# RWKV layer of a fused four-mixer kernel: another order for the first pairs' steps beside the projection, and for the solve's rows in the pair loop

## The reference

```python
r, k, v, g = jnp.einsum('pbsd,pdf->pbsf', xs[:4], w_in)
w_log = -jax.nn.softplus(-(w0 + jnp.tanh(xw @ w1) @ w2)) - 0.5
a = jax.nn.sigmoid(a0 + (xa @ a1) @ a2)
kk = kk / jnp.maximum(jnp.linalg.norm(kk, axis=-1, keepdims=True), 1e-12)
k = k * (1.0 + (a - 1.0) * k_a)
def step(state, inp):
    r_t, w_t, k_t, v_t, kk_t, a_t = inp
    sk = jnp.einsum('bhvk,bhk->bhv', state, kk_t)
    state = state * w_t[:, :, None, :] - sk[..., None] * (kk_t * a_t)[:, :, None, :] + v_t[..., None] * k_t[:, :, None, :]
    return state, jnp.einsum('bhvk,bhk->bhv', state, r_t)
bonus = jnp.sum(rh * kh * r_k, axis=-1, keepdims=True) * vh
```

## Time and profile before

| | |
|---|---|
| runs of the kernel before | 3641.15, 3643.06, 3659.37 us; median 3643.06 |
| the profiled execution | 3642.96 us, its span 3641.3 us |
| PE busy in the span | 3447.9 us, 95% |
| DVE, ACT, POOL busy | 1989.7, 1702.4, 252.7 us |
| granted TensorE clock, mean | 0.975 |

### The profile page before, as it was taken

One profiled execution on the slowest core, in us unless ns is written; L12 is line 12 of the kernel. 1 busy time (PEld: TensorE's weight loads), 2 busy tenths in 40 slices (PEclk: granted clock), 3 DMA queues, 4 the chain that ended last, 5 costly groups with the idle time before them and its releaser, 6 DMA issues. The chain is left out here.

```text
span 3641.3 us, 48005 instructions
## 1 busy us (share of the span) xinstructions
PE 3447.9 (95%) x18610; PEld 2851.4 (78%) x18610; DVE 1989.7 (55%) x3850; ACT 1702.4 (47%) x3234; POOL 252.7 (7%) x194
## 2 busy tenths in 40 slices
PE   7999898999998999999899899999899999999999
PEld 6888646877886777777787688888778888888887
DVE  3144343354335686775434477777864566666562
ACT  3222363265444454543324466666642765665530
POOL 0011130000001122212000000000100000000100
PEclk9999999999999999999899999999999999999899
DMA  4333403112232222222411111111222211111231
GB/s 146 121 128 128 167 1 127 41 64 81 96 107 88 73 59 62 67 56 53 148 57 42 51 36 36 36 36 36 78 86 70 93 35 41 41 36 47 70 110 47
DMA packets 219482, 263.70 MB, mean 72 GB/s; under 512 B 62716, under 2 KB 143092, under 8 KB 218232
## 3 DMA queue, kind: packets, MB, share of 16 engines
q1 hardware_dynamic: 219256, 260.63, 22.2%
HBM read 190.58 MB, written 69.99 MB: 72 GB/s over the span
## 5 line engine op out<-in xcount | busy, mean ns | idle before, releaser
L332 PE MATMUL bank<-wh,XH 128*128 128x512 f32 x1344 | 536.2, 399 | 13.2 <-DVE wl L316 9.5
L332 PE MATMUL bank<-wh,XL 128*128 128x512 f32 x1344 | 528.2, 393 | 0.0
L332 PE MATMUL bank<-wl,XH 128*128 128x512 f32 x1344 | 528.1, 393 | 0.0
L2706 PE MATMUL bank<-XH,wh 128*128 128x512 f32 x1040 | 424.5, 408 | 10.1 <-DVE wl L2695 9.6
L2706 PE MATMUL bank<-XH,wl 128*128 128x512 f32 x1040 | 408.7, 393 | 0.0
L2706 PE MATMUL bank<-XL,wh 128*128 128x512 f32 x1040 | 408.2, 392 | 0.0
L332 PEld LDWEIGHTS bank<-wh,XH 128*128 128x128 f32 x1344 | 255.7, 190 | 65.9 <-issue 10.3
L316 DVE TENSOR_TENSOR wl<-raw,wh 128x1024 fp32r<-128x1024 f32 x128 | 160.9, 1269 | 266.7 <-ACT wh L307 265.9
L332 PEld LDWEIGHTS bank<-wl,XH 128*128 128x128 f32 x1344 | 255.3, 190 | 54.3
L332 PEld LDWEIGHTS bank<-wh,XL 128*128 128x128 f32 x1344 | 255.9, 190 | 50.4
L332 PE MATMUL bank<-XH,wh 128*128 128x512 f32 x704 | 280.9, 399 | 6.8 <-DVE XL L1598 6.0
(11 more groups left out here) (441 smaller groups left out, 6902.0 us busy)
## 6 DMA issues: line engine op xcount, KB each, us to landing
sc_zt<-stage SPq DMA_DIRECT2D x88, 256.0 KB, 2.0
raw<-in_att_w_in SPq DMA_DIRECT2D x33, 512.0 KB, 4.2
raw<-in_even_w_in SPq DMA_DIRECT2D x32, 512.0 KB, 5.2
raw<-in_odd_w_in SPq DMA_DIRECT2D x32, 512.0 KB, 4.6
raw<-in_rec_w_in SPq DMA_DIRECT2D x32, 512.0 KB, 4.0
sc_h<-H SPq DMA_DIRECT2D x24, 512.0 KB, 2.6
sc_z<-stage SPq DMA_DIRECT2D x40, 256.0 KB, 2.0
z<-sc_z SPq DMA_DIRECT2D x8, 1024.0 KB, 5.6
```

Of the source, the lines that this page charges most:

```text
L332: done = e.matmul(out, lhsT, rhs, start=k == 0 and j == 0, stop=k == NK - 1 and j == 2)
L2706: done = e.matmul(bank[:, :], x[:, k, :], y[:, k, ts], start=k == 0 and j == 0, stop=k == NK - 1 and j == 2)
```

## The change

No arithmetic changes, and no DMA or instruction is added or removed. Two tables are rewritten; POOL's product inside `key` gets a step name of its own, `grow`, which stands right behind `key` wherever `key` stood, so that POOL's order stays as it was.

Beside the projection: `keys` of pair 0 goes from slot 2 to 0, its `scan` from 2 to 3 (behind `norm`), `lora` 0 of pair 1 from 8 to 5, `pack` 1 from 8 to 7, `bonus` of pair 0 from 10 to 11, `load` of pair 1 from 10 to 11, `centre` of pair 1 from 12 to 11. The solve's rows of pair 0 stood 5, 7, 7, 7, 5 in slots 9 to 13 and stand 4, 11, 1, 3, 7, 5 in slots 8 to 13.

In the pair loop: the rows stood 1, 4, 1, 3, 4, 2, 3, 6, 3, 4 at positions 5, 6, 7, 8, 9, 10, 11, 13, 14, 15 and stand 1, 4, 3, 5, 2, 3, 4, 9 at 5, 6, 8, 9, 10, 11, 13, 14. `bonus` goes behind the four rows of position 6, and `gates` from 7 to 6.

```diff
-    6: ((-1, 'tail', 1, 5), (1, 'bonus'), (1, 'solve', 4)),
-    7: ((1, 'solve', 1), (0, 'gates')),
+    6: ((-1, 'tail', 1, 5), (1, 'solve', 4), (1, 'bonus'), (0, 'gates'), ),
+    7: (),
...
-    13: ((1, 'solve', 4), (0, 'tail', 0, 1), (1, 'solve', 2)),
-    14: ((2, 'norm'), (1, 'solve', 3)),
-    15: ((0, 'tail', 0, 2), (1, 'solve', 4)),
+    13: ((1, 'solve', 4), (0, 'tail', 0, 1), ),
+    14: ((2, 'norm'), (1, 'solve', 3), (1, 'solve', 2), (1, 'solve', 4), ),
+    15: ((0, 'tail', 0, 2), ),
...
-        if what == "key":
+        if what == "grow":
             e.wait_ge(*self.scaled.at("rate", p))
             e.tensor_tensor(k, k, t, ALU.mult).then_inc(*self.key.up("k", p))
```

More of the change, by code:

```diff
@@ L1724 @@
 PLACED = {
[L1725 to L1730, removed]
-    6: ((-1, 'tail', 1, 5), (1, 'bonus'), (1, 'solve', 4)),
-    7: ((1, 'solve', 1), (0, 'gates')),
[L1733 to L1736, removed]
+    0: ((1, 'rh'), (1, 'alike', 1), (-1, 'tail', 1, 0), ),
+    1: ((-1, 'tail', 1, 1), ),
+    2: ((1, 'alike', 2), (-1, 'tail', 1, 2), (1, 'rkr'), ),
+    3: ((1, 'alike', 3), ),
+    4: ((1, 'pack', 0), (-1, 'tail', 1, 3), ),
+    5: ((-1, 'tail', 1, 4), (1, 'pack', 1), (2, 'load'), (1, 'solve', 1), ),
+    6: ((-1, 'tail', 1, 5), (1, 'solve', 4), (1, 'bonus'), (0, 'gates'), ),
+    7: (),
+    8: ((2, 'lora', 0), (1, 'solve', 3), ),
+    9: ((1, 'solve', 5), ),
+    10: ((2, 'keys'), (1, 'solve', 2), ),
+    11: ((0, 'tail', 0, 0), (2, 'lora', 1), (2, 'scan'), (1, 'solve', 3), ),
     12: (),
-    13: ((1, 'solve', 4), (0, 'tail', 0, 1), (1, 'solve', 2)),
-    14: ((2, 'norm'), (1, 'solve', 3)),
-    15: ((0, 'tail', 0, 2), (1, 'solve', 4)),
+    13: ((1, 'solve', 4), (0, 'tail', 0, 1), ),
+    14: ((2, 'norm'), (1, 'solve', 3), (1, 'solve', 2), (1, 'solve', 4), ),
+    15: ((0, 'tail', 0, 2), ),
     16: (),
[L1742 to L1748, removed]
+    17: ((1, 'unpack'), (2, 'spread'), (0, 'tail', 0, 3), (2, 'centre'), ),
+    18: ((2, 'unit'), ),
+    19: ((2, 'key'), (2, 'grow'), (2, 'exps'), ),
+    20: ((0, 'tail', 0, 4), ),
+    21: ((2, 'be'), (2, 'al'), ),
+    22: ((2, 'ka'), (0, 'tail', 0, 5), ),
+    23: ((2, 'values'), (2, 'alike', 0), ),
 }
@@ L1803 @@
 HALVES = (slice(0, 512), slice(512, 1024))
[L1807 to L1817, removed]
+BESIDE = {
+    -4: ((0, 'load'), ),
+    -1: ((0, 'begin'), (0, 'tables'), ),
+    0: ((0, 'lora', 0), (0, 'keys'), ),
+    1: ((0, 'lora', 1), ),
+    2: (),
+    3: ((0, 'norm'), (0, 'spread'), (0, 'scan'), (0, 'centre'), ),
+    4: ((0, 'unit'), (0, 'key'), (0, 'grow'), ),
+    5: ((0, 'exps'), (1, 'lora', 0), (0, 'be'), (0, 'al'), ),
+    6: ((0, 'alike', 0), (0, 'alike', 1), (0, 'alike', 2), (0, 'alike', 3), (0, 'pack', 0), ),
+    7: ((0, 'pack', 1), ),
+    8: ((0, 'rest'), (0, 'values'), (0, 'blank'), (0, 'ka'), (0, 'rh'), (0, 'rkr'), (0, 'solve', 4), ),
+    9: ((0, 'solve', 11), ),
+    10: ((0, 'solve', 1), (1, 'lora', 1), ),
+    11: ((0, 'solve', 3), (1, 'keys'), (1, 'scan'), (1, 'load'), (1, 'centre'), (0, 'bonus'), ),
+    12: ((0, 'solve', 7), (1, 'norm'), (1, 'spread'), ),
+    13: ((0, 'solve', 5), (0, 'unpack'), (1, 'unit'), ),
+    14: ((1, 'key'), (1, 'grow'), (1, 'exps'), ),
+    15: (),
+}
+PROLOGUE = ((1, 'values'), (0, 'gates'), (0, 'tokens', 0), (0, 'scores', 0), (0, 'level', 0, 'X'), (0, 'level', 0, 'G'), (0, 'level', 0, 'Y'), (0, 'level', 0, 'F'), (1, 'be'), (1, 'al'), (1, 'ka'), (1, 'alike', 0), )
 def rwkv_beside():
```

## The result

The kernel after takes 3629.26 us (median of 13 runs, 3620.31 to 3633.39), beside 3646.19 for the kernel before on the same chip. By the medians that is 16.9 us. The ratio of the means is 0.9946, 95% interval 0.9932 to 0.9959: 0.54% faster, 19.7 us of 3643. In a second comparison (`after_again`) it was 0.9956 [0.9941, 0.9971]. The profiled execution took 3621.33 us and is the second fastest of the 13.

A forecast was written before the change was run, and what follows sets the result against it. PE, busy 95% of the span, was taken to bound the kernel through its idle time beside the projection and in the pair loop. 12.1 + 1.2 + 5.8 = 19.1 us off 3642.96 gave 3624, range 3612 to 3638.

The forecast's parts named there:

- Beside the projection: Ahead of the pair loop: `unit` of pair 1 starts 12.1 us earlier, and 1.2 us of clock come back behind it.
- DVE's queue: Beside the projection: DVE needs 24.45 us from 1171.0, the end of `rkr`, to the floor of pair 1, at 1195.4.
- POOL's hold: Beside the projection: DVE's products of two SBUF tensors stand still while POOL's run; one row took 2.29 us.
- The new stop: Beside the projection: PE waits 4.4 us ahead of `norm` of pair 1 for the first DVE half of `bonus`.
- The clock behind `unit`: Behind `unit` of pair 1: part of the time lost at the lower clock returns, 0 to 2.4 us, taken as 1.2.
- The other moves cost nothing.: Beside the projection: `keys`, `scan` and `lora` 0 go into idle time of ACT and PE, at no cost.
- The pair loop, 5.8: Pair loop: `T` 0.60 us earlier in five pairs gives 3.0, and 1.4 each in two others 2.8.
- rival (a): Pair loop gives nothing: `S` is only late elsewhere, its DMA eats `T`'s 0.6; 3629.7 us, chance 0.20.
- Rival (c): Pair loop: the clock falls more with 2.3 us waited ahead of chunk 6, costing 12; 3636 us, chance 0.14.
- the larger of two gaps decides: Pair loop: the larger wait, 2.3 against 2.0 us, sets the clock's falls, a little worse than before.
- (b): POOL holds DVE less, r lands earlier; DVE starts up to 4.6 us earlier or clock stays up; about 3613, chance 0.13.
- (d): Pair loop: each pair loses half of a 13.5 us low-clock stretch, 47 us less 9.6; 3661 us, chance 0.03.

The follow-up runs named there:

- after_again: The kernel after, unchanged, profiled and compared with the kernel before a second time: ratio 0.9956.
- e3_keys_scan: The kernel after with `keys` and `scan` of pair 0 back in their old places beside the projection: ratio to the kernel before 0.9975.
- e1_beside: The kernel after with the pair loop's table and prologue as before, so only the order beside the projection is new: ratio to the kernel before 0.9996.
- e6_row7: The kernel after with positions 6, 7 and 9 of the pair loop as before: ratio to the kernel before 0.9966.
- e7_bonus_later: The kernel before with `lora` 1 of pair 1 ahead of `bonus` of pair 0, which heads slot 11: ratio to the kernel before 0.9996.
- before_again: The kernel before, unchanged, profiled a second time: its pair loop took 545.6 us again.
- e8_best: The kernel after with k's load in slot 9, `bonus` in slot 10 and nine rows behind the gate of tile (7,5): ratio to the kernel before 0.9960.
- e9_split: The kernel after with only one of the two rows moved behind the S of chunk 5 in the pair loop: ratio to the kernel before 0.9959.
- e10_fill: As e8_best, but the last nine rows stand ahead of the gate of tile (7,5): 3619.57 us, ratio to the kernel before 0.9931.
- e2_loop: The kernel before with the new pair loop's table and prologue, the order beside the projection old: ratio to the kernel before 0.9985.

## Why the prediction was right, and where it wasn't

**The total.** Forecast 3624 against a profiled 3642.96, 19 us; measured 19.7 by the first ratio, 16.0 by the second. It is right, but the terms are not. Beside the projection 16.6 and 14.5 us came for the 13.3 forecast, from the loop -0.3 and -1.4 for 5.8, and 5.2 and 3.1 ahead of and behind both, where nothing had been forecast. That these add up to the forecast is luck.

**DVE's queue** (24.45 us from `rkr` to the floor): 24.37. POOL's hold: the prediction read one row of 2.29 as a full stop. Both products of row 4 now last 2.17 and 2.50 us, against 0.28 and 0.29 for the same shapes alone, and end with POOL's. The prediction had put row 4 ahead of POOL; it did not fit in, at no cost. The ten rows behind it were not slowed, because POOL was done. The Trainium skill, "GPSIMD Engine Reference", section "8. Key points", speaks of contention with two-input DVE instructions; the trace agrees, and shows it as a standstill for the whole of POOL's product.

**The new stop** ahead of `norm`: 4.4 forecast, 3.62 measured. Keys were forecast 1.3 us ahead of the bank; their squares end at 1181.51 + 1.13 = 1182.64 and the first half of `bv` at about 1182.32 + 0.64 = 1182.96, 0.3 ahead. In `after_again` the squares end the wait, which is 3.61 as well. So the cover was as good as gone, at no cost.

**The clock behind `unit`**, 1.2 forecast: from `unit` to X(0,0) it was 16.0 and 15.8 us before, 14.6 and 15.6 after, so 1.4 in the first pair of profiles and 0.2 in the second.

**"The other moves cost nothing."** This is one of the two steps that failed. The prediction held the start of DVE's queue at 1171.0 "since r is still loaded behind the gate of tile (7,0)". The gate itself moved: `keys` and `scan` of pair 0 took away a wait of 0.85 ahead of `norm` and, where the clock then stayed up, what it cost behind. By `e3_keys_scan` that is 2.6 to 5.0 us. SP issues the load of r 57.1 us behind `lora` 1 of pair 0 before, 53.4 and 56.2 in the two profiles after, 59.1 in `e3_keys_scan`. `rkr` ends 5.9 us earlier, 4.4 with the 1.4 of the start off (in `after_again` 1.7); and X(0,0) came 14.5 to 16.6 us earlier and not 13.3. The move of `lora` 0 did cost nothing.

**The pair loop, 5.8.** This is the other step. Between before and after it gave nothing (545.6 twice, then 545.9 and 547.0): rival (a)'s figure. But rival (a)'s reason isn't right. The r waits came out as forecast (0.45 and 2.45 for 0.5 and 2.3), T's waits shrank by more than forecast, and on the old start the new table gives 3.4 us in the profile and 5.5 by the ratio. What failed is the addition: both terms were priced against the kernel before, whose old loop keeps the clock up for most pairs (42 to 49 us at 0.50). With the start moved, the old loop is at 0.50 for 86 and 106 us, in two profiles that took 6 and 9 us longer than the mean of their kernels. Against the 564.1 of `e1_beside` the new loop is worth 17 to 18 us; (106 - 65) / 2 = 20 us, an estimate of what the matmuls at 0.50 take too long, is enough for all of it. By the ratios, 0.9996 against 0.9946 and 0.9956, it is 15 to 18 us, of which 3 to 5 stand ahead of X(0,0) already. The ratios alone show that the two halves do not add: 0.04% and 0.15% alone, 0.44 to 0.54% together, where the intervals of the three leave some 0.2% to either side of the difference. Rival (c), that the clock turns against the wait of 2.45, got its place right: in the first six pairs of both profiles after, 3.4 to 6.8 us at 0.50 lie around the wait ahead of chunk 6. Its price of 12 was too high, but the mechanism is large enough to have eaten the 5.8: 61 and 69 us at 0.50 in the new loop against 49 and 42 in the old cost 6 to 14 us by half of the difference (an estimate). So the figure is (a)'s and the mechanism, as far as two profiles of each kernel tell, (c)'s. The Trainium skill, "TensorE: Matmul & The Clock Gate", section "HAM oscillation — how this bites in real kernels", warns of idle gaps that return the array to half clock; the traces agree that this is what the loop pays. The prediction's reading of it, that the larger of two gaps decides, does not hold: see the last part.

**Rivals (b) and (d).** An earlier start of DVE was (b)'s, and an earlier r too; but r came earlier mainly because its load was issued 3.7 us earlier; from that issue to POOL's start 4.8 us passed in place of 5.6, and that much at most can be `pn` out of its way. POOL was no softer. (d)'s 47 us did not come; `e1_beside` shows the mechanism, at 18 us in its profile and about 10 on average. Some 3.7 us of each profile's difference lie in the rest behind the loop, where no instruction moved. Two profiles of one kernel differ there by 3.3 (before) and 3.5 us (after), so these need not come from the change.

**Open.** Why the clock falls for 17.1 us around the r of chunk 3: six times in `e1_beside`, `e6_row7` and `e7_bonus_later` (waits of 0.60 to 0.94 us in five places, 1.83 in one), once in `before_again` (0.60), and once each in `e8_best` and `e9_split` (0.32, with the stop for `bonus` just ahead). The same r waits 0.60 in most pairs of the two profiles of before, and 1.18 in the first, without it. The size of the wait alone doesn't tell, since `e9_split`, too, speaks against it. Whether it is the distance between the waits, how densely PE works between them, or merely when the wait comes, no run here separates. The prediction had `bonus` behind the four rows done in time for that `lora`; it was not in `e8_best`, `e9_split` and `e10_fill` (waits of 0.34 to 1.15), where it was in the two profiles after.

## What to carry to other kernels

Price a change at two places together, and against a kernel that has the other half: here 1.5 and 5.5 us alone were 16 to 20 together. Ahead of a queue's start ask what its own first cover hangs on; a move "into idle time" upstream shifts it. And when a stop goes, look at which engine idles next: `e8_best` took the stop ahead of `norm` away and won nothing, `e10_fill` put DVE's rows into its idle 4.8 us besides and won. Last, a profile is one execution: see where it stands among the runs of its kernel before a time read from it is called the order's.

## What the hardware showed that I had not expected

The wait ahead of the first X(0,0) goes with the clock of the next 10 us in every profile, unlike the waits of the loop. With 1.33 us ahead of it (1.31 in one), as with every other wait there followed by two of 0.7 and about 0.5, the clock was down for 6.7 to 13.6 us in each of six profiles; with 2.3 (`e3_keys_scan`, `after_again`) for 17, with 5.28 for 20.5. With 0.24 it stayed at 1.00 in `before`, `before_again`, `e7_bonus_later` and `e10_fill`, and with 0.36 in `e2_loop`; in four of these five the clock had already been down some 10 us ahead, around the longer stop for `unit`. No run changed this wait alone, so the two go together and neither is shown to be the cause. The kernel after, in the stretch where it was down:

```profile
1214.00:1224.20 10.20, 10.20 (x52) 8.86 (x48) 3.20 (x8) 1.58 (x5) 5.47 (x5) 0.52 0.38 146
```

In the loop a wait of 2.45 was followed by 3.4 to 6.8 us at 0.50, and one of 0.66 by 17. Executions of one program spread over 7 to 28 us, and 6 to 13 of them gave intervals of 0.10 to 0.16% to either side: a difference under 0.2% between two kernels isn't told here.
